# A three-block kernel's first mixer put in step order, its scan inputs ahead of q, with the shifted norms turned tile by tile and products of ones in TensorE's waits

## Chip, cores and metric

One NeuronCore of one Trainium2 chip. The metric is the device time of one execution in microseconds (us); lower is better. All data are float32, batch 1, 256 tokens, width 1024.

## The reference, cut to what matters

Nine stages run one after the other on one X of 256 x 1024: feed-forward, first mixer, feed-forward, feed-forward, second mixer, feed-forward, feed-forward, third mixer, feed-forward. The first three are normalized and then scaled and *shifted* by vectors computed from `c`; the later six have a plain norm. The change touches the three shifted norms and the first mixer.

```python
h = modulate(rms_norm(x, g_pre_mix), sh2, sc2)      # h * (1 + scale) + shift
proj = h @ w_in                                     # q 512, k 128, v 128, u 512 columns
attn = sliding_window_attention(q, k, v, sinks)     # 8 heads of 64, window 128
# state space: 32 groups of 16 channels, each a complex diagonal state of 64
bu = einsum('bsgh,gph->bsgp', u, b_bar)
states = associative_scan(a * left + right)         # over the 256 steps
y = real(einsum('bsgp,ghp->bsgh', states, c_mat)) + u * d_skip
y = gelu(y);  y = y * sigmoid(y @ w_glu + b_glu)
mixed = concat(rms_norm(attn, g_attn_out), rms_norm(y, g_ssm_out)) @ w_out
x = x + ga2 * rms_norm(mixed, g_post_mix)           # ga2: the gate of this block
```

## The kernel before, in words

**Panels.** The weights stream through a ring of six slots as panels of 128 x 1024 (`raw`). SyncE loads a panel as soon as VectorE has split the one that had its slot. ScalarE rounds it to `w_hi` (`split_hi`, line 185), VectorE takes the rest, `w_lo` (`split_lo`, line 191), and TensorE makes each product as three: hi by hi, hi by lo, lo by hi (`product3`, line 207). Activations are split alike, `h_hi` and `h_lo`. The order of the panels is fixed by hand in `stream_of_panels`, and the order in which each engine splits them, relative to its other work, is written out by hand in each stage. M1 is the mixer's first panel: 0 to 3 are u, 4 is k, 5 to 8 are q, 9 is v, 10 and 11 the GLU's weights, 12 to 19 `w_out`.

**The norm.** `add_dve` (lines 715 and 722) adds a stage's result to X; ScalarE takes squares (line 302), GpSimd the power -1/2 (lines 337, 338), VectorE writes one diagonal matrix for each half of the tokens (`diag_dve`, line 376), and `norm_turn_pe` (line 414) transposes and scales X by a matmul with the diagonal: for the first half of the tokens all eight channel tiles, then for the second half. ScalarE writes `h_hi` from PSUM with scale and shift (`norm_act_rest`, line 330), VectorE first the same in float32 into `h32` and then `h_lo` (`low_dve`, lines 394 and 396). Both wait for tiles by pairs, since two tiles share a PSUM bank. TensorE begins the first panel tile by tile as `h_lo` comes (`norm_pe`, `first_channels`, `first_up`).

**The first mixer.** TensorE (`mix1_pe`): u's first panel, projection 1, the gate of this block (`gate_pe`: ones times `acc_gate_1`, line 835, which VectorE's `gate_dve` takes up), projections 2 to 4; then four rounds of: projection 5 + b, `input_pe(b)` (line 1496, four groups of states by 64 blocks of four steps), scores of two heads (`attention_pe`, lines 1458 and 1459, banks 0 and 1); then `output_pe(0)` (lines 1506 and 1509), projection 9 (v) and its transposes (line 1538), `output_pe(1)`; then per head the transposes of the probabilities (line 1470) and the products with v (lines 1482 to 1484), with `output_pe(2)` and (3) in between. ScalarE copies each projection out (lines 1595 to 1599), gathers u by the four steps of a block into `u_steps` (`step`, line 1607, reading every fourth float), takes exponentials (line 1619), copies the turned probabilities (line 1627) and applies the Gelu (line 1633, writing every fourth float of `y32`), two groups of it ahead of `probabilities(4)`. VectorE: splits, `gate_dve`, then four times `states_dve` (lines 1742 to 1751: rotate, scan), biases and maxima of two heads (lines 1758 and 1762), a split. GpSimd turns the states back (lines 1715 to 1720), the third and fourth time only when `output_pe` has read the first and second. Then come `attention_out` (line 1788), `y_lo` (line 1813), the GLU product, Sigmoid (line 1674), the transposes of the attention, and eight `out_product`, with the sum of the gated squares (line 1568) behind the second and the row of factors (line 1440) behind the third.

Of the kernel before, what the change touches and what calls it, by code (L numbers as in the profile page):

```python
# [81 lines left out]
def build_program(nc, panels, ada, cols, rows, sinks, ssm_mats, skip, tables, pool_mats, rope, near,  # L82
                  pool_w, decay, mlp_w, feats, x_in, out, spectrum, last_stage):
    ctx = ExitStack()
    with ctx:
# [193 lines left out]
        PLAIN = 3  # L279

# [127 lines left out]

        def norm_turn_pe(pe, n):

            for m in range(MT):
                pe.wait_ge(diag_done, 2 * n + m + 1)
                for k in range(KT):
                    mm = pe.matmul(turned_out(n, k)[:, m * P:(m + 1) * P], X[:, m, k * P:(k + 1) * P],  # L414
                                   diag[:, m, :], start=True, stop=True)
                    if m == MT - 1:
                        mm.then_inc(turned, 1)

        def norm_pe(pe, n, first):
# [942 lines left out]
        u_steps = region(5120, STATE_TILES, BLOCKS)  # L1362
# [6 lines left out]
        p_turned = region(0, 2, 384)  # L1369
# [79 lines left out]
        def attention_pe(pe, i):  # L1449
# [5 lines left out]
            pe.wait_ge(m1_evac, 6 + j)  # L1455
# [57 lines left out]
        def mix1_pe(pe):  # L1513
# [23 lines left out]
            for m in range(MT):  # L1537
                tr = pe.transpose(bank[4][:, m * P:(m + 1) * P], v_t[:, m * P:(m + 1) * P], ident[:, :])
            tr.then_inc(v_turned, 1)
            output_pe(pe, 1)  # L1540
            pe.wait_ge(v_ready, 1)
            for i in range(8):
# [3 lines left out]
                if i == 3:  # L1546
                    output_pe(pe, 2)
                if i == 5:
# [13 lines left out]
            out_product(0)  # L1562
            out_product(1)
# [20 lines left out]

        def by_query(row, half, wide=2):
# [3 lines left out]
        def mix1_act(act, order):  # L1589
            def project(j):  # L1590
# [3 lines left out]
                if j < 4:  # L1594
                    ins = act.activation(u_t[:, j, :], src, ACT.Copy)
                elif 5 <= j < 9:
                    ins = act.activation(q_t[:, j - 5, :], src, ACT.Copy, scale=HD ** -0.5)
                else:
                    ins = act.activation(k_t if j == 4 else v_t, src, ACT.Copy)
                ins.then_inc(m1_evac, 1)  # L1600

            def step(b):
                if b == 0:
                    act.wait_ge(m1_evac, 4)
                    act.wait_ge(gate_sums, 4)
                for j in range(STEP):
                    act.activation(u_steps[32 * j:32 * j + 32, 4 * b:4 * b + 4, :],
                                   u_t[32 * b:32 * b + 32, :, :].rearrange("p q (t j) -> p q t j", j=STEP)[:, :, :, j],
# [40 lines left out]
            act.wait_ge(v_turned, 1)  # L1649
            act.activation(v_tok[:, :, :].rearrange("p m c -> p (m c)"), bank[4][:, 0:SEQ],  # L1650
                           ACT.Copy).then_inc(v_ready, 1)
# [1103 lines left out]
```

## Time and profile before

| | |
|---|---|
| median of 3 runs | 1647.46 us (1646.73 to 1650.32) |
| the profiled execution | 1646.31 us, its span 1644.2 us |
| mean granted TensorE clock | 0.964 of 2.4 GHz |
| TensorE matmul, weight load | 94%, 86% of the span |
| VectorE, ScalarE, GpSimd | 62%, 47%, 13% |
| chain that ended last | TensorE 83%, VectorE 8%, ScalarE 4%, issue 2%, DMA 1% |
| DMA | 293.24 MB, 178 GB/s over the span |

How to read it: the span runs from the first to the last instruction of one execution; the execution's own time is 2.1 us longer. Matmul times are pipelined and overlap (a record of 0.28 us can follow another after 0.12). One float32 matmul shows as two records. Times in a timeline are us from the span's start. The clock is the share of full speed that TensorE was granted: 1.00 is 2.4 GHz, 0.50 is 1.2 GHz.

### The profile page before, as it was taken

To read this page: it belongs to the slowest core of one execution; us is meant where nothing else is said; L and a number is where in the kernel's file an instruction comes from. 1 tells how busy PE (TensorE), PEld (TensorE's weight loads), DVE (VectorE), ACT (ScalarE), POOL (GpSimd) and SP (SyncE) were. 2 spreads that over 40 slices of the span, in tenths; PEclk is the share of its full clock that TensorE was granted. 3 is DMA by queue.
4 is the path that set the end of the run, shared out by engine and by line. 5 is a ranking of instruction groups with operands and counts; after the bars stand their busy time and mean duration, and the time that the engine had idled before them with its cause. 6 is when DMAs were issued, how large, how long until landed. Compare 5 with 4: busy or idle time off the path is not lost.

```text
span 1644.2 us, 27917 instructions
## 1 busy us (share of the span) xinstructions
PE 1539.4 (94%) x10274; PEld 1407.5 (86%) x10274; DVE 1024.8 (62%) x1379; ACT 767.7 (47%) x1211; POOL 212.9 (13%) x254
## 2 busy tenths in 40 slices
PE   3989998968899999999999999999999988999997
PEld 3989987867898888999988799999999978899996
DVE  6997776724765556655556765556655558565554
ACT  2345534654545445544454354444544456354443
POOL 1593191221101111000000000000000000000000
PEclk8999988968999999999999999999999999999999
DMA  9887863203565553855533345553655532245551
GB/s 350 303 293 273 277 254 130 81 26 128 189 199 191 205 192 118 302 188 191 191 129 105 123 158 186 190 191 131 215 191 189 177 108 102 77 167 191 190 185 47
DMA packets 80287, 293.24 MB, mean 178 GB/s; under 512 B 9035, under 2 KB 9388, under 8 KB 79644
## 3 DMA queue, kind: packets, MB, share of 16 engines
q1 hardware_dynamic: 75728, 274.97, 48.8%
q0 software_dynamic: 3712, 15.16, 2.6%
q10 hardware_dynamic: 780, 2.18, 0.5%
q8 instruction: 46, 0.75, 0.2%
q14 instruction: 21, 0.17, 0.0%
HBM read 289.13 MB, written 3.15 MB: 178 GB/s over the span
## 4 chain that ended last, share of the span: by engine, by line
PE 83%; DVE 8%; ACT 4%; issue 2%; DMA 1%; POOL 1%; SPq 0%; DVEq 0%; ACTq 0%
PE bank L207 73%; DVE w_lo L191 2%; DVE arena L774 1%; PE bank L1904 1%; PE bank L1200 1%; ACT arena L302 1%; PE bank L1917 1%; ACT w_hi L185 1%; PE bank L811 1%; PE bank L405 1%; DMA raw<-panels 1%; PE bank L1509 1%; PE bank L414 1%; DVE arena L715 1%; PE bank L1096 0%
## 5 line engine op out<-in xcount | busy, mean ns | idle before, releaser
L207 PE MATMUL bank<-h_hi,w_hi 128*128 128x256 f32 x2376 | 689.6, 290 | 17.1 <-DVE h_lo L396 5.5
L207 PE MATMUL bank<-h_lo,w_hi 128*128 128x256 f32 x2376 | 678.6, 286 | 0.0
L207 PE MATMUL bank<-h_hi,w_lo 128*128 128x256 f32 x2376 | 678.3, 285 | 0.0
L191 DVE TENSOR_TENSOR w_lo<-raw,w_hi 128x1024 fp32r<-128x1024 f32 x458 | 552.1, 1253 | 126.8 <-ACT w_hi L185 126.1
L207 PEld LDWEIGHTS bank<-h_hi,w_hi 128*128 128x128 f32 x2376 | 462.3, 195 | 35.7 <-DVE h_lo L396 7.6
L185 ACT ACTIVATE w_hi<-raw 128x1024 fp32r<-128x1024 f32 x458 | 457.4, 1049 | 65.0 <-PE bank L207 33.0
L207 PEld LDWEIGHTS bank<-h_lo,w_hi 128*128 128x128 f32 x2376 | 462.6, 195 | 6.1 <-issue 2.2
L207 PEld LDWEIGHTS bank<-h_hi,w_lo 128*128 128x128 f32 x2376 | 462.0, 194 | 0.0
L618 DVE TENSOR_TENSOR arena<-arena,bank 128x256 f32<-128x256 f32 x132 | 55.3, 419 | 249.7 <-PE bank L207 180.0
L207 PE MATMUL bank<-w_hi,f_hi 128*128 128x512 f32 x528 | 207.6, 393 | 0.2 <-DVE f_lo L623 0.2
L207 PE MATMUL bank<-w_hi,f_lo 128*128 128x512 f32 x528 | 207.0, 392 | 0.0
L207 PE MATMUL bank<-w_lo,f_hi 128*128 128x512 f32 x528 | 205.5, 389 | 0.0
L555 ACT ACTIVATE f_hi<-arena 128x256 fp32r<-128x256 f32 x132 | 55.1, 418 | 251.7 <-DVE arena L618 251.7
L337 POOL TENSOR_SCALAR stat<-stat 128x1 f32<-128x1 f32 x26 | 10.8, 417 | 1015.5 <-ACT arena L302 1014.7
L549 ACT ACTIVATE arena<-arena 128x256 f32<-128x256 f32 x88 | 36.8, 418 | 195.5 <-DVE arena L612 195.5
L207 PEld LDWEIGHTS bank<-w_lo,f_hi 128*128 128x128 f32 x528 | 99.2, 188 | 21.7
L207 PEld LDWEIGHTS bank<-w_hi,f_hi 128*128 128x128 f32 x528 | 99.6, 189 | 17.9 <-issue 0.4
L207 PEld LDWEIGHTS bank<-w_hi,f_lo 128*128 128x128 f32 x528 | 99.6, 189 | 15.7
L774 DVE SCALAR_TENSOR_TENSOR arena<-arena,stat 128x1024 f32<-128x1024 f32 x70 | 94.2, 1345 | 3.4 <-DMA arena<-ada 1.8
L623 DVE TENSOR_TENSOR f_lo<-arena,f_hi 128x256 fp32r<-128x256 f32 x132 | 59.9, 454 | 50.8 <-ACT f_hi L555 50.8
L553 ACT ACTIVATE arena<-bank 128x256 f32<-128x256 f32 x44 | 16.8, 383 | 146.3 <-PE bank L207 146.1
L207 PE MATMUL bank<-w_hi,h_hi 128*128 128x512 f32 x116 | 49.2, 424 | 7.0 <-DVE h_lo L1824 2.8
(315 smaller groups left out, 1310.0 us busy)
## 6 DMA issues: line engine op xcount, KB each, us to landing
raw<-panels SPq DMA_DIRECT2D x458, 512.0 KB, 4.7
arena<-ada SPq DMA_DIRECT2D x64, 512.0 KB, 5.2
arena<-ada POOLq DMA_DIRECT2D x8, 512.0 KB, 3.9
arena<-rows POOLq DMA_DIRECT2D x4, 512.0 KB, 4.2
spectrum<-arena POOLq DMA_DIRECT2D x2, 1024.0 KB, 7.4
arena<-spectrum POOLq DMA_DIRECT2D x1, 2048.0 KB, 19.4
X<-x_in SPq DMA_DIRECT2D x1, 1024.0 KB, 5.4
arena<-decay ACTq DMA_DIRECT2D x2, 512.0 KB, 5.7
```

The lines of the kernel that those rows point to most:

```text
L185: act.activation(w_hi[:, slot, :], raw[:, slot, :], ACT.Copy).then_inc(hi_ready, 1)
L191: dve.tensor_tensor(w_lo[:, slot, :], raw[:, slot, :], w_hi[:, slot, :].bitcast(F32), ALU.subtract).then_inc(lo_ready, 1)
L207: last = pe.matmul(out_ap, a, b, start=start and n == 0, stop=stop and n == 2)
L302: return act.activation(squares[:, q, :], source, ACT.Square, scale=D ** -0.5, accum_out=stat[:, at + q:at + q + 1])
L405: tr = pe.transpose(turned_out(n, k)[:, m * P:(m + 1) * P], X[:, m, k * P:(k + 1) * P], ident[:, :])
L414: mm = pe.matmul(turned_out(n, k)[:, m * P:(m + 1) * P], X[:, m, k * P:(k + 1) * P], diag[:, m, :], start=True, stop=True)
L549: act.activation(ffn_buf[:, f % 2, :], gate_buf[:, f % 2, :], ACT.Silu).then_inc(silu_done, 1)
L553: act.activation(ffn_buf[:, f % 2, :], gate_out(at, f), ACT.Silu).then_inc(silu_done, 1)
L555: act.activation(f_hi[:, f % 2, :], ffn_buf[:, 2 + f % 2, :], ACT.Copy).then_inc(f_hi_done, 1)
L618: dve.tensor_tensor(ffn_buf[:, 2 + f % 2, :], ffn_buf[:, f % 2, :], up_out(at, f), ALU.mult).then_inc(hidden_done, 1)
L623: dve.tensor_tensor(f_lo[:, f % 2, :], ffn_buf[:, 2 + f % 2, :], f_hi[:, f % 2, :].bitcast(F32), ALU.subtract).then_inc(f_lo_done, 1)
L774: dve.scalar_tensor_tensor(out=dst, in0=src, scalar=c, in1=dst, op0=ALU.mult, op1=ALU.add).then_inc(ada_used, 1)
```

## The change

In the shifted norms `norm_turn_pe` turns X tile by tile (both halves of the tokens of one tile, then the next), and for tiles 2, 4 and 6 ScalarE, not VectorE, writes the float32 copy `h32`. Ahead of the turns of the second and third norm TensorE multiplies 24 times ones by ones into bank 7, and in the second norm once more after each of the first seven tiles, into bank 3. In the mixer `u_t`, `y32` and what follows them stand in the order of the four steps, so that the copy out of u writes with a stride of 64 floats, and the gathering copies and the Gelus run over contiguous floats; VectorE's product `gated_y` goes back to token order, and moves from behind the first `m_lo` to ahead of it. VectorE gathers group 0, ScalarE groups 1 to 3. The q projections 5 to 8 become q, q, v, q, q (panels 5, 6, 7, 8, 9), `input_pe(0)` and (1) and `output_pe(0)` and (1) move, v's transposes go to bank 7. On ScalarE the last four probabilities stand ahead of all Gelus. The gate's two matmuls move from behind projection 1 to behind `out_product(0)`, and `gate_dve` behind the splits 16 and 17. Three of VectorE's splits move behind the second maxima.

```diff
@@ norm
+        BY_ACT = (2, 4, 6)
...
                 act.wait_ge(turned, of_channel(n, k))
+                if sh is not None and k in BY_ACT:
+                    act.activation(h32[:, k, :], turned_out(n, k), ACT.Identity, scale=sc[:, k:k + 1],
+                                   bias=sh[:, k:k + 1])
...
-                    order(dve.tensor_scalar(h32[:, k, :], ps, sc[:, k:k + 1], sh[:, k:k + 1],
-                                            ALU.mult, ALU.add))
+                    if k not in BY_ACT:
+                        order(dve.tensor_scalar(h32[:, k, :], ps, sc[:, k:k + 1], sh[:, k:k + 1],
+                                                ALU.mult, ALU.add))
...
+        def keep_busy(pe, to, times):
+            for _ in range(times):
+                pe.matmul(bank[to][:, 0:P], ones[:, :], ones[:, :], start=True, stop=True)
...
         def norm_turn_pe(pe, n):
-            for m in range(MT):
-                pe.wait_ge(diag_done, 2 * n + m + 1)
-                for k in range(KT):
+            if n:
+                keep_busy(pe, 7, 24)
+            for k in range(KT):
+                for m in range(MT):
+                    if k == 0:
+                        pe.wait_ge(diag_done, 2 * n + m + 1)
...
                 first(k)
+                if n == 1 and k < KT - 1:
+                    keep_busy(pe, 3, 1)
@@ mix1_pe
             norm_pe(pe, 1, first_channels)
-            m1_projection_pe(pe, 1)
-            gate_pe(pe, 1, acc_gate_1, (6, 7))
-            for j in range(2, 5):
+            for j in range(1, 5):
                 m1_projection_pe(pe, j)
-            for b in range(4):
-                m1_projection_pe(pe, 5 + b)
-                input_pe(pe, b)
-                attention_pe(pe, 2 * b)
-                attention_pe(pe, 2 * b + 1)
+            input_pe(pe, 0)
+            m1_projection_pe(pe, 5)
+            attention_pe(pe, 0)
+            attention_pe(pe, 1)
+            m1_projection_pe(pe, 6)
+            input_pe(pe, 1)
+            attention_pe(pe, 2)
+            attention_pe(pe, 3)
+            m1_projection_pe(pe, 7)
+            m1_projection_pe(pe, 8)
+            input_pe(pe, 2)
             output_pe(pe, 0)
+            attention_pe(pe, 4)
+            attention_pe(pe, 5)
+            pe.wait_ge(m1_evac, 8)
+            for m in range(MT):
+                tr = pe.transpose(bank[7][:, m * P:(m + 1) * P], v_t[:, m * P:(m + 1) * P], ident[:, :])
+            tr.then_inc(v_turned, 1)
             m1_projection_pe(pe, 9)
+            input_pe(pe, 3)
+            output_pe(pe, 1)
+            attention_pe(pe, 6)
+            attention_pe(pe, 7)
             pe.wait_ge(m1_evac, 10)
-            for m in range(MT):
-                tr = pe.transpose(bank[4][:, m * P:(m + 1) * P], v_t[:, m * P:(m + 1) * P], ident[:, :])
-            tr.then_inc(v_turned, 1)
-            output_pe(pe, 1)
...
-                if i == 3:
+                if i == 1:
                     output_pe(pe, 2)
-                if i == 5:
+                if i == 4:
                     output_pe(pe, 3)
...
             out_product(0)
+            pe.wait_ge(sig_done, 4)
+            gate_pe(pe, 1, acc_gate_1, (6, 7))
             out_product(1)
@@ mix1_act
-                    ins = act.activation(u_t[:, j, :], src, ACT.Copy)
+                    ins = act.activation(u_t[:, j, :].rearrange("p (j t) -> p t j", j=STEP),
+                                         src.rearrange("p (t j) -> p t j", j=STEP), ACT.Copy)
...
-                        y32[32 * b:32 * b + 32, :, :].rearrange("p q (t i) -> p q t i", i=STEP)[:, :, :, i],
+                        y32[32 * b:32 * b + 32, :, :].rearrange("p q (i t) -> p q i t", i=STEP)[:, :, i, :],
...
-            step(0)
+            act.wait_ge(u_stepped, 4)
+            step(1)
             project(4)
-            step(1)
+            step(2)
             project(5)
-            step(2)
             step(3)
-            for j in range(6, 9):
+            for j in (6, 7, 8):
                 project(j)
+            act.wait_ge(v_turned, 1)
+            act.activation(v_tok[:, :, :].rearrange("p m c -> p (m c)"), bank[7][:, 0:SEQ],
+                           ACT.Copy).then_inc(v_ready, 1)
             exps(0)
             project(9)
...
             exps(1)
-            gelu(0)
-            gelu(1)
-            probabilities(4)
-            probabilities(5)
-            gelu(2)
-            probabilities(6)
-            gelu(3)
-            probabilities(7)
+            for i in range(4, 8):
+                probabilities(i)
+            for b in range(4):
+                gelu(b)
@@ mix1_dve
-            for j in range(3):
+            for j in range(4):
                 split_lo(dve, M1 + 3 + j)
-            gate_dve(dve, 1, (6, 7), order)
-            for j in range(3, 5):
-                split_lo(dve, M1 + 3 + j)
+            dve.wait_ge(m1_evac, 4)
+            for j in range(STEP):
+                dve.tensor_copy(u_steps[32 * j:32 * j + 32, 0:4, :], of_step(0, j)).then_inc(u_stepped, 1)
+            split_lo(dve, M1 + 7)
...
-                split_lo(dve, M1 + 8 + s)
+                if s < 2:
+                    split_lo(dve, M1 + 8 + s)
             maxima(1)
-            split_lo(dve, M1 + 12)
+            for j in range(10, 13):
+                split_lo(dve, M1 + j)
...
+            for n in range(4):
+                dve.wait_ge(sig_done, n + 1)
+                dve.tensor_tensor(gated_y[:, n, :].rearrange("p (t i) -> p i t", i=STEP),
+                                  gate_in[:, n, :].rearrange("p (i t) -> p i t", i=STEP),
+                                  y32[:, n, :].rearrange("p (i t) -> p i t", i=STEP), ALU.mult).then_inc(gated, 1)
...
             dve_panels(dve, M1 + 16, 2)
+            gate_dve(dve, 1, (6, 7), order)
```

## Rows read from the trace of the kernel before

**Rows 1.** Chain of waits, 260 to 424 us: start, length, what

```profile
286.65 1.72 PE bank L835 x4
...
288.37 11.51 PE bank L207 x96
...
299.88 1.75 PE bank L1496 x16
...
369.01 8.32 PE bank L207 x48
```

**Rows 2.** Windows: us, busy of PE, PEld, DVE, ACT, POOL, clock, DMA share, GB/s

```profile
263.50:268.30 4.80, 0.00 (x0) 0.00 (x0) 4.17 (x7) 3.26 (x11) 2.25 (x5) 1.00 0.26 96
274.90:278.50 3.60, 2.48 (x12) 1.66 (x12) 3.46 (x9) 2.63 (x5) 0.00 (x0) 1.00 0.00 0
278.60:285.50 6.90, 6.90 (x28) 6.26 (x29) 4.95 (x8) 1.33 (x2) 2.10 (x2) 0.51 0.23 76
319.60:323.00 3.40, 2.77 (x21) 2.29 (x21) 3.16 (x11) 3.34 (x10) 0.00 (x0) 1.00 0.00 0
323.10:329.20 6.10, 6.10 (x28) 5.45 (x27) 5.86 (x10) 2.84 (x11) 0.00 (x0) 0.50 0.30 89
334.50:345.00 10.50, 10.25 (x92) 9.96 (x92) 1.38 (x3) 6.05 (x23) 3.91 (x4) 1.00 0.16 58
351.80:366.30 14.50, 12.20 (x54) 11.43 (x54) 0.00 (x0) 7.91 (x14) 0.00 (x0) 0.50 0.00 1
410.70:416.00 5.30, 0.00 (x0) 0.00 (x0) 4.42 (x8) 3.40 (x11) 2.65 (x6) 0.93 0.00 0
```

**Rows 3.** Timeline around the two later norms: start, length, engine, line, operation

```profile
269.68 0.29 DVE L376 TENSOR_SCALAR diag<-ident,stat 128x128 f32<-128x128 f32 x1 [0.85 <-POOL stat L338]
...
272.82 3.76 ACT L330 ACTIVATE h_hi<-bank,mods,pre_scale 128x256 fp32r<-128x256 f32 x8 [4.37 <-PE bank L414]
...
273.88 0.54 DVE L394 TENSOR_SCALAR arena<-bank,pre_scale,mods 128x256 f32<-128x256 f32 x1 [3.91 <-ACT h_hi L330]
...
281.20 1.22 DVE L191 TENSOR_TENSOR w_lo<-raw,w_hi 128x1024 fp32r<-128x1024 f32 x1
...
416.87 1.60 DVE L376 TENSOR_SCALAR diag<-ident,stat 128x128 f32<-128x128 f32 x1 [0.85 <-POOL stat L338]
...
420.75 2.39 ACT L330 ACTIVATE h_hi<-bank,mods,pre_scale 128x256 fp32r<-128x256 f32 x5 [5.11 <-PE bank L414]
...
430.29 0.39 ACT L553 ACTIVATE arena<-bank 128x256 f32<-128x256 f32 x1 [2.58 <-PE bank L207]
```

**Rows 4.** Timeline of the mixer's loop, VectorE and GpSimd

```profile
301.75 1.42 DVE L1742 TENSOR_TENSOR arena<-bank,arena 128x512 f32<-128x512 f32 x2 [2.08 <-PE bank L1496]
...
305.31 0.53 DVE L1758 SCALAR_TENSOR_TENSOR arena<-arena,bank 128x384 f32<-128x384 f32 x1
...
309.01 1.40 DVE L1742 TENSOR_TENSOR arena<-bank,arena 128x512 f32<-128x512 f32 x2
...
309.63 0.73 POOL L1720 TENSOR_TENSOR arena<-arena 128x256 f32<-128x256 f32 x1
```

**Rows 5.** Timeline of TensorE: two heads' scores; from one head's values to the next

```profile
315.41 0.50 PE L1458 MATMUL bank<-arena 64*128 64x128 f32 x4
...
316.28 0.39 PE L207 MATMUL bank<-h_hi,w_hi 128*128 128x256 f32 x1
...
339.16 0.50 PE L1470 MATMUL bank<-ident,arena 128*128 128x128 f32 x3
...
340.12 0.50 PE L1470 MATMUL bank<-ident,arena 128*128 128x128 f32 x3
```

**Rows 6.** ScalarE's groups (busy us, mean ns, idle before) and the Gelus' table load

```profile
L1633 ACT ACTIVATE arena<-bank 32x256 f32<-32x256 f32 x16 | 9.8, 612 | 6.7 <-PE bank L1509 6.4
...
L553 ACT ACTIVATE arena<-bank 128x256 f32<-128x256 f32 x44 | 16.8, 383 | 146.3 <-PE bank L207 146.1
...
344.90 1.28 ACT L1633 ACT_TABLE_LOAD   x1
```

More of the change, by code:

```diff
@@ L407, in turn_pe @@
                 tr.then_inc(turned, 1)
+        def keep_busy(pe, to, times):
+            for _ in range(times):
+                pe.matmul(bank[to][:, 0:P], ones[:, :], ones[:, :], start=True, stop=True)
         def norm_turn_pe(pe, n):
[L411 to L413 removed]
+            if n:
[4 more added lines that the diff above has]
+                        pe.wait_ge(diag_done, 2 * n + m + 1)
                     mm = pe.matmul(turned_out(n, k)[:, m * P:(m + 1) * P], X[:, m, k * P:(k + 1) * P],
                                    diag[:, m, :], start=True, stop=True)
[L416 to L417 removed]
+                mm.then_inc(turned, 1)
         def norm_pe(pe, n, first):
@@ L1361, in build_program @@
         q_t = region(1024, 4, SEQ)
-        u_steps = region(5120, STATE_TILES, BLOCKS)
+        u_steps = region(0, STATE_TILES, BLOCKS)
         y32 = region(4096, 4, SEQ)
@@ L1368, in build_program @@
         turned_states = (region(8704, 2, SEQ), region(9216, 2, SEQ))
-        p_turned = region(0, 2, 384)
+        p_turned = region(10752, 2, 384)
+        gated_y = region(11264, 4, SEQ)
         attn = region(3072, 2, 512)
@@ L1454, in attention_pe @@
             b = bank[i % 2]
-            pe.wait_ge(m1_evac, 6 + j)
+            pe.wait_ge(m1_evac, (6, 7, 9, 10)[j])
             if i >= 2:
@@ L1583, in turn_attention_pe, with of_step @@
                     tr.then_inc(attn_turned, 1)
+        def of_step(b, j):
+            return u_t[32 * b:32 * b + 32, :, :].rearrange("p q (j t) -> p q j t", j=STEP)[:, :, j, :]
         def by_query(row, half, wide=2):
@@ L1594, in project @@
                 if j < 4:
-                    ins = act.activation(u_t[:, j, :], src, ACT.Copy)
-                elif 5 <= j < 9:
-                    ins = act.activation(q_t[:, j - 5, :], src, ACT.Copy, scale=HD ** -0.5)
+                    ins = act.activation(u_t[:, j, :].rearrange("p (j t) -> p t j", j=STEP),
+                                         src.rearrange("p (t j) -> p t j", j=STEP), ACT.Copy)
+                elif j in (4, 7):
+                    ins = act.activation(k_t if j == 4 else v_t, src, ACT.Copy)
                 else:
-                    ins = act.activation(k_t if j == 4 else v_t, src, ACT.Copy)
+                    ins = act.activation(q_t[:, (5, 6, 8, 9).index(j), :], src, ACT.Copy, scale=HD ** -0.5)
                 ins.then_inc(m1_evac, 1)
             def step(b):
-                if b == 0:
-                    act.wait_ge(m1_evac, 4)
-                    act.wait_ge(gate_sums, 4)
                 for j in range(STEP):
-                    act.activation(u_steps[32 * j:32 * j + 32, 4 * b:4 * b + 4, :],
-                                   u_t[32 * b:32 * b + 32, :, :].rearrange("p q (t j) -> p q t j", j=STEP)[:, :, :, j],
+                    act.activation(u_steps[32 * j:32 * j + 32, 4 * b:4 * b + 4, :], of_step(b, j),
                                    ACT.Copy).then_inc(u_stepped, 1)
@@ L1686, in mix1_act @@
                 act.wait_ge(gated, n + 1)
-                act.activation(y_squares[:, n, :], gate_in[:, n, :], ACT.Square).then_inc(gsq_done, 1)
+                act.activation(y_squares[:, n, :], gated_y[:, n, :], ACT.Square).then_inc(gsq_done, 1)
             act_panels(act, M1 + 18, 2)
@@ L1825, in mix1_dve @@
                                   ALU.subtract).then_inc(m_lo, 1)
-            for n in range(4):
-                dve.wait_ge(sig_done, n + 1)
-                dve.tensor_tensor(gate_in[:, n, :], gate_in[:, n, :], y32[:, n, :],
-                                  ALU.mult).then_inc(gated, 1)
             dve_panels(dve, M1 + 16, 2)
+            gate_dve(dve, 1, (6, 7), order)
             dve.wait_ge(gsum_done, 1)
@@ L1836, in mix1_dve @@
             for n in range(4):
-                dve.scalar_tensor_tensor(out=h32[:, 4 + n, :], in0=gate_in[:, n, :],
+                dve.scalar_tensor_tensor(out=h32[:, 4 + n, :], in0=gated_y[:, n, :],
                                          scalar=col("g_ssm", n), in1=bank[4][:, 0:SEQ], op0=ALU.mult,
@@ L2610, in mix1 @@
         q = w[:, :512].reshape(D, 2, 4, HD).transpose(0, 2, 1, 3).reshape(D, 512)
-        return [columns(w[:, 768:]), columns(w[:, 512:640]), columns(q), columns(w[:, 640:768]),
+        return [columns(w[:, 768:]), columns(w[:, 512:640]), columns(q[:, 0:256]), columns(w[:, 640:768]),
+                columns(q[:, 256:]),
                 together(columns(a["ssm_w_glu"][0]), 2), a["w_out"][0].reshape(8, P, D)]
```

3 lines of the change are left out of this document (removed).

## The prediction

> **What bounds the kernel now.** I read the page's share of busy time first (TensorE 94%), then the chain of waits, the windows, and the timeline of each engine from 262 to 431 us, the part that the diff touches. Past it TensorE multiplies almost without a break, so what is gained before passes to the end one for one. In the chain [rows 1] the reader is to see four projections in 11.51 us, 2.88 each, then `input_pe(0)`, 16 records in 1.75, and the GLU product only at 369.01: 67 us lie between. In the windows [rows 2] the granted clock is 0.50, the 1.2 GHz level, in 278.6 to 285.5, 323.1 to 329.2 and 351.8 to 366.3, each time after a stretch in which TensorE had gaps. The norm [rows 3] is paced by VectorE: eight tiles from 273.88 to 281.20, 0.915 each. The mixer's loop is VectorE's too [rows 4]: 301.75 to 309.01, 7.26 a step, of which the states take 3.56, two heads 2.3, a split 1.4. Last, two groups of Gelus stand on ScalarE ahead of probabilities that TensorE waits for.
>
> **The norm ahead of the mixer.** The turn went token half by token half, so ScalarE began at 272.82, with tiles 0 and 1 whole. Now these need six records after the second diagonal, ready at 269.68 + 0.29 [rows 3]. A float32 matmul is two records, and the gate's two took 1.72 as four records of 512 columns [rows 1], 0.107 per 128 columns. 270.0 + 0.64 + 0.15 to drain: ScalarE starts at 270.8. It needs 3.76 for eight tiles, about 0.45 each; with three copies more it ends at 275.9. VectorE starts 1.05 after it, as now, and loses three instructions of 0.57 (273.88 to the next in the pair): 271.9 + 7.3 - 1.7 = 277.5 for the last `h_lo`, and ScalarE is never later than it wants. TensorE ends projection 0 at 278.0.
>
> The 24 products of ones are 48 records, 5.1 us at the full clock. They fill an idle time (263.5 to 268.3: no TensorE [rows 2]); at the half clock they would take 10.2 and end 4.9 late. The single product in each later wait costs 0.21 and stands in waits of 0.3 to 0.5; where ScalarE made the copy the tile comes after 0.35 and it may delay 0.2, which the next tile gives back. I take it that all this holds the clock: the fall at 278.5 came after 3.6 us in which TensorE was busy for 2.48. Without the half clock, and without the gate's 1.72, projections 1 to 4 run from 278.0 to 289.5 and `input_pe(0)` to 291.3, where it ended at 301.6: 10.3 gained. The group 0 copies of u, now VectorE's, are ready at about 288.5 (projection 3 ends at 286.65, ScalarE's copy out takes 0.4 to 0.65, VectorE's four 0.2 to 0.4 each); projection 4 hides them with 1 us in hand, and beyond that they would cost one for one. ScalarE's copy of u now writes with a stride, between 0.38 and 0.61 each [rows 6]; it stands beside projections of 2.88 and costs nothing.
>
> **The loop.** ScalarE waits for VectorE's copies (288.5); behind that wait stand its step 1 and split 7, so VectorE's split 7 ends at 292.2 and the first states begin there, 9.5 earlier. From here the two engines alternate. TensorE: projection 5 to 294.2, two heads after the copy of q, 0.87 (315.41 to 316.28 [rows 5]), projection 6, `input_pe(1)`: 300.3. VectorE: step 0 to 299.5, step 1 from 300.3, heads done 306.2, split 307.6. TensorE: heads, projections 7 and 8, `input_pe(2)`: 300.3 + 0.9 + 5.76 + 1.75 = 308.7; `output_pe(0)` (24 records of 0.11) 2.6, heads 0.9, v 0.4, projection 9, `input_pe(3)`: 317.3. VectorE: states(3) to 320.9, two heads to 323.3. GpSimd turns a group of states 4.9 after its scan (305.4 to 310.36 [rows 4]); it waits for `output_pe(0)` before group 2, and that now ends at 311.3, ahead of states(2): no `output_pe` waits. SyncE refills a slot when VectorE has split it: splits 10 to 12 move behind the maxima, to 327 to 330, and their loads are for panels used after 360. ScalarE's wait for v holds up the Exps to 314.4; they end at 318.2, q's last copy at 319.7, and TensorE comes for it at 320.0.
>
> **The values.** TensorE has two heads to turn, and then nothing until the eighth head leaves the score banks at 323.3. What follows are `output_pe(2)` and (3), 2.6 each, and eight heads of values at 0.96 (339.16 to 340.12 [rows 5]): 12.9, with waits the last product at 336.7. At 1.2 GHz the same is 5.2, 5.2 and eight times 1.92, less 0.7 done before the gap, with waits of 1: the last product at about 347.5. Nearest rows [rows 2]: 319.6 to 323.0, busy 2.77 of 3.4 with narrow products, and 0.50 straight after; 351.8 to 366.3, busy 12.2 of 14.5, stayed at 0.50. Against them 334.5 to 345.0 held 1.00, but without gaps (10.25 of 10.5). With a gap of near 2 us I take the half clock. The Trainium skill (TensorE: Matmul & The Clock Gate, section Why this matters for your kernels) asks only that TensorE have no long idle gap between bursts; by that rule the clock stays full here, the last product is at 336.7 and the total 1622. The window at 319.6 speaks against it: no long gap stood there and the clock fell.
>
> **The Gelus.** They come last: a table load 1.28, then 16 at 612 ns as now, or 383 as a ScalarE function of 256 contiguous elements out of PSUM [rows 6]; the diff makes their writes contiguous, so I take the nearer row, 383, back to back 0.33: 5.3 in all. Bounds: 4.8 and 10.2 (0.64 each, today's spacing). With `y_hi`, two of 512 columns at 0.6 (between once and twice 383), and two `y_lo` of 0.35 behind it: 345.5 + 1.3 + 5.3 + 1.2 + 0.8 = 354.1 for the GLU, against 369.01. **Gain 14.9.** It contains the 10.3 of the front.
>
> **The tail.** The gate's 1.72 now stands behind `out_product(0)`, on TensorE's way to the sum of squares, the row and the last products: **cost 1.7**, nothing hides it. Its wait for the Sigmoids is over by then. VectorE's gating moves ahead of `m_lo`; it needs 0.5 after the last Sigmoid (bounds 0.42 and 0.65 for its strided write), and `m_hi` comes over 1 us later.
>
> **The second norm.** Here the second diagonal took 1.60 [rows 3], beside GpSimd's load and memset, so 418.5. ScalarE can start at 419.25, against 420.75. Then TensorE's 48 products (5.8) are slower than VectorE's tiles: first Silu at 427.6 against 430.29, gain 2.7 at the full clock. But here TensorE goes idle at 410.7 (410.7 to 416.0: nothing [rows 2]), the ones end 5.1 later, and nearly 3 us with little to do follow; a fall there costs 2.4 of the 2.7. I take **1.5**. The first norm gains nothing: its six products a tile last longer at the half clock (1.28) than VectorE's 0.915.
>
> **Sum.** -14.9 + 1.7 - 1.5 = -14.7. The profiled execution took 1646.31: 1631.6. The median is 1.15 higher, so **1632.5 us**.
>
> **Rivals.** *Full clock in the values*: GLU at 344.5, 24.5 earlier; +1.7, -2.7: -25.5, 1622. The window 334.5 to 345.0 is for it. So is the rule of the Trainium skill named above. Chance 0.20. *The Gelus stay at 0.64*, because of their 32 partitions or the function: +4.9, 1637. The trace has no contiguous one. 0.13. *An earlier fall*, between 307 and 321: a projection, an input and an output at half, 2.9 + 1.75 + 2.6, less waits: +5, 1637.5. 0.15. *Slower than before*: the half clock comes with `input_pe(0)` at 289.5 and stays to the GLU. Five projections cost 14.4 more, four inputs 7.0, two outputs 5.2, four pairs of heads 3.5; less 3 of waits, 27: -14.7 + 27, 1660. It turns the sign once more than 15 of these 27 are paid. Against it: four projections in a row ran at the full 2.88 after just such a half stretch [rows 1]. 0.04. *Nothing comes of it*: GpSimd or the Exps take VectorE's place, within 3 us. 0.02.
>
> **Numbers.** My own case has 0.46 and spans 1628 to 1636. For 8 in 10 the range goes to the full clock on one side, and on the other to where a dear Gelu or an early fall comes with a late wait or two: 1621 to 1641. A measurement of this kernel tells 0.2%, 3.3 us, from no change. Faster 0.94, within 0.02, slower 0.04.
>
> **What would show it.** Right: clock 1.00 from the mixer's first product to about 320 and 0.50 from 323 to the GLU; the first `h_hi` 2 us earlier; `input_pe(0)` over by 291.5; the Gelus at 0.38; GLU at 354; a step of 1.7 behind `out_product(0)`. Wrong: a wait for VectorE or ScalarE ahead of a projection between 292 and 317, products of ones at 0.21 a record, or values at 0.11 per narrow record.

## The result, and the profile after

The changed kernel takes **1636.33 us** in the median of four runs (1634.08 to 1638.84); the kernel before, run beside it, 1647.86 (1646.73 to 1650.32). The ratio is 0.9929 (95% interval 0.9916 to 0.9942): 11.5 us faster. Two executions of this case, one of `no_ones` (3020.16 us) and one of the kernel before (2171.43), fell in a much slower state and are left out everywhere. The forecast was 1632.5 in a range of 1621 to 1641; the prediction's own case spans 1628 to 1636, and the median lies 0.3 above it. The execution shown below took 1634.08 (span 1632.3), 12.2 less than the one shown of before.

The page of the changed kernel: its busy time by engine, and the granted clock in 40 slices.

```profile
PE 1542.5 (94%) x10384; PEld 1415.1 (87%) x10384; DVE 1024.4 (63%) x1374; ACT 762.8 (47%) x1216; POOL 211.4 (13%) x254
...
PEclk7999989959999999999999999999999988999999
```

The shares tell nothing: TensorE was and is 94% busy. The clock row does: the ninth slice (327 to 367 us) is at 5, and two slices of the last mixer (1306 to 1388) are at 8.

The chain of waits of the changed kernel, from the first mixer's norm to the second norm (start us, us, what), the lines that answer to [rows 1, 3]:

```profile
270.22 0.30 DVE diag L380
...
270.57 3.62 PE bank L427 x30
...
278.48 9.10 PE bank L207 x75
...
287.61 0.65 ACT arena L1626
...
299.78 1.73 PE bank L1511 x16
...
314.02 1.17 DVE arena L1797
...
315.21 1.30 DVE arena L1799 x2
316.53 0.72 DVE arena L1801
...
322.08 0.27 ACT arena L1631
...
325.23 0.41 PE bank L1497 x2
...
345.99 1.28 ACT L1661
...
355.81 8.55 PE bank L207 x48
...
372.58 1.72 PE bank L849 x4
...
386.67 9.19 PE bank L207 x39
...
404.09 1.61 DVE diag L380
...
405.75 5.24 PE bank L427 x30
```

The reader is to see the GLU product at 355.81 instead of 369.01 [rows 1], the gate's 1.72 at 372.58 in the tail, and VectorE's operations of four and eight elements of `maxima(0)` (L1797 to L1801), 1.3 us a pair where the same pair of L1799 takes 0.23 in `maxima(1)`, in the chain to the last copy of q (L1631), for which TensorE waited.

The windows of the changed kernel (columns as in [rows 2]):

```profile
318.00:322.40 4.40, 3.24 (x31) 3.11 (x29) 4.16 (x8) 4.34 (x17) 0.00 (x0) 1.00 0.00 0
322.40:327.30 4.90, 3.88 (x33) 3.33 (x33) 4.45 (x9) 0.87 (x2) 3.91 (x4) 1.00 0.00 0
327.30:348.00 20.70, 20.08 (x98) 19.70 (x96) 4.23 (x8) 8.51 (x26) 0.00 (x0) 0.50 0.22 77
348.00:355.80 7.80, 0.00 (x0) 0.00 (x0) 2.72 (x7) 7.43 (x19) 0.00 (x0) 0.50 0.00 1
355.80:361.50 5.70, 5.69 (x26) 5.69 (x27) 4.25 (x5) 4.53 (x8) 2.50 (x4) 0.50 0.50 172
...
405.90:409.30 3.40, 3.40 (x17) 3.40 (x18) 0.93 (x3) 1.33 (x3) 1.07 (x2) 0.51 0.65 213
```

From the norm to 327.3 the clock is 1.00; from there through all the values, the wait for the Gelus and most of the GLU it is 0.50, the 1.2 GHz level.

Kernels whose code ahead of this part is the same start it up to 6.4 us apart in their profiles (`norm_only` at 259.67, `early_q` at 266.07), since the part ahead of it varies. So I compare stages by their length, each the difference of two times of the timeline: first square of the feedforward's result (A), last `h_lo` of the mixer's norm (B), end of `input_pe(0)` (C), second product of the first head's values, in `attention_out_pe(0)` (D; the first product starts 0.24 us earlier in the changed kernel), last value product (E), GLU product (F), first square behind the mixer (G), first Silu (H). The kernels of the section on experiments stand in the same table, one profiled execution each.

| kernel | A-B | B-C | C-D | D-E | E-F | F-G | G-H | A-H |
|---|---|---|---|---|---|---|---|---|
| before | 19.84 | 20.32 | 37.11 | 27.50 | 2.79 | 39.66 | 21.62 | 168.84 |
| changed | 16.24 | 13.92 | 33.30 | 22.43 | 7.91 | 40.07 | 20.90 | 154.77 |
| norm_only | 16.27 | 18.51 | 35.49 | 27.51 | 2.80 | 39.72 | 20.89 | 161.19 |
| mixer_only | 20.58 | 13.93 | 33.96 | 13.82 | 8.92 | 39.29 | 21.62 | 152.12 |
| no_ones | 17.87 | 13.93 | 34.23 | 24.25 | 7.93 | 40.81 | 21.54 | 160.56 |
| fill_wait | 16.26 | 13.91 | 33.30 | 17.99 | 7.94 | 37.44 | 20.89 | 147.73 |
| gate_front | 16.26 | 15.64 | 33.29 | 13.83 | 8.90 | 37.47 | 21.18 | 146.57 |
| gate_front_no_ones | 17.88 | 15.63 | 33.29 | 22.74 | 7.92 | 39.63 | 20.88 | 157.97 |
| ones_front | 16.24 | 15.71 | 34.23 | 24.25 | 7.91 | 39.28 | 19.27 | 156.89 |
| gelu_stride | 16.26 | 13.93 | 33.30 | 22.71 | 11.71 | 39.62 | 20.73 | 158.26 |
| early_q | 16.25 | 13.93 | 31.26 | 18.11 | 7.91 | 39.49 | 20.76 | 147.71 |
| early_fill | 16.25 | 13.93 | 31.63 | 17.45 | 8.44 | 35.93 | 20.85 | 144.48 |
| best | 16.24 | 15.64 | 31.64 | 13.42 | 6.95 | 35.78 | 20.89 | 140.56 |
| best_no_fill | 16.26 | 15.64 | 31.25 | 13.42 | 6.39 | 40.07 | 20.89 | 143.92 |

Between A and H the change is worth 14.1 us. The profile shown started A 0.56 later than that of before, so 13.5 were left at the first Silu (416.78 against 430.29), and 11.9 of the span at the end. The rest was given back far behind the change. Windows of the changed kernel and then of the kernel before, where the last mixer runs at the half clock:

```profile
1334.50:1344.60 10.10, 6.77 (x30) 6.48 (x31) 6.79 (x11) 4.63 (x5) 0.00 (x0) 0.50 0.15 54
1361.70:1371.90 10.20, 9.29 (x27) 7.21 (x27) 6.66 (x13) 5.35 (x15) 0.00 (x0) 0.50 0.01 2
```

```profile
1350.50:1357.30 6.80, 3.75 (x18) 3.46 (x17) 5.16 (x9) 4.63 (x5) 0.00 (x0) 0.50 0.12 25
1418.70:1422.10 3.40, 3.30 (x13) 3.00 (x13) 2.69 (x5) 1.90 (x4) 0.00 (x0) 0.50 0.00 0
```

The code there is the same; 20 us at the half clock stand against 10. By the chain the changed kernel was 14.85 ahead at the first products of that mixer (1324.75 against 1339.60) and 11.87 at its last norm (1430.72 against 1442.59). All fourteen traces of this case hold this unchanged code. From the row of factors ahead of those products to the turn of that norm, its length goes with its time at the half clock: 103.6 us in the kernel before (10.2 us at 0.50), 104.0 to 104.8 in four others (13.7 or 17.1 us), 106.5 to 106.9 in the nine with 20.5 us, the changed kernel among them.

### The profile page after: what moved, and what is told of

Its sections match the earlier page's. It is cut to its first block, busy times and chain, and to the rows that moved or that the text cites. A ratio compares the mean times of both kernels' runs of the same rounds, so it can differ in the third digit from the quotient of the medians.

```text
span 1632.3 us, 28136 instructions
## 1 busy us (share of the span) xinstructions
PE 1542.5 (94%) x10384; PEld 1415.1 (87%) x10384; DVE 1024.4 (63%) x1374; ACT 762.8 (47%) x1216; POOL 211.4 (13%) x254
## 4 chain that ended last, share of the span: by engine, by line
PE 83%; DVE 7%; ACT 4%; issue 2%; DMA 1%; POOL 1%; SPq 0%; DVEq 0%; ACTq 0%
PE bank L207 73%; DVE w_lo L191 2%; DVE arena L788 1%; PE bank L1933 1%; PE bank L1214 1%; DMA arena<-ada 1%; ACT arena L303 1%; ACT w_hi L185 1%; PE bank L2262 1%; PE bank L1946 1%; POOL stat L342 1%; PE bank L410 1%; PE bank L427 1%; PE bank L2284 1%; PE bank L825 1%
```

## The experiments

Twelve kernels ran, those of one group on one chip with the kernel before between them (its medians there: 1646.32 to 1648.86), so that kernels of two groups compare better by their ratios and stages than by their medians. All compute the whole reference; a product of ones is one whose result nobody reads. The ratios are as recorded; where times fall in two groups, they can differ from the quotient of the medians (0.9915 for `no_ones`).

| kernel | median us (runs) | ratio to before, 95% interval |
|---|---|---|
| changed | 1636.33 (4) | 0.9929, 0.9916 to 0.9942 |
| no_ones | 1633.55 (6) | 0.9900, 0.9885 to 0.9914 |
| norm_only | 1638.09 (5) | 0.9942, 0.9930 to 0.9955 |
| mixer_only | 1634.62 (6) | 0.9925, 0.9908 to 0.9943 |
| fill_wait | 1631.83 (5) | 0.9906, 0.9892 to 0.9920 |
| gate_front | 1626.78 (4) | 0.9878, 0.9861 to 0.9896 |
| gelu_stride | 1641.18 (1) | one run, no interval |
| early_q | 1630.02 (4) | 0.9895, 0.9878 to 0.9913 |
| early_fill | 1625.60 (4) | 0.9879, 0.9861 to 0.9897 |
| ones_front | 1634.28 (6) | 0.9914, 0.9892 to 0.9936 |
| gate_front_no_ones | 1640.17 (6) | 0.9950, 0.9934 to 0.9965 |
| best | 1620.72 (5) | 0.9835, 0.9819 to 0.9851 |
| best_no_fill | 1623.33 (5) | 0.9850, 0.9836 to 0.9863 |

**The change in two halves.** `norm_only` is the kernel before with the norm's part of the diff (`BY_ACT`, `keep_busy`, `norm_turn_pe`, `norm_pe`) and nothing else; `mixer_only` the changed kernel without that part.

> The kernel before with the norm part of the change alone (turn tile by tile, ScalarE's copies for tiles 2, 4, 6, products of ones). Theory A (front first): the last h_lo near 277.5, the clock held at 1.00 through the first projections, some 7 us gained before input_pe(0) that old loop passes on, and 1 to 2 at the norm behind the mixer: 1639 to 1641. Theory B (the old order of the mixer, paced by VectorE's gate and splits, eats it): 2 to 4 us gained, 1644 to 1646, and the mixer part holds the rest.

> The changed kernel with the norms as they were before (token half by token half, no copies by ScalarE, no products of ones). Theory A: the clock falls near 268 and 278 as before, the front loses about 7 us against the changed kernel, the second norm 1.5 to 2.5: 1643 to 1645. Theory B (the step order carries the gain): 1638 to 1641.

Measured: 9.4 us gained by the norm alone and 12.9 by the mixer alone, while both together gave 11.5. They do not add. The table shows why. The norm's part is worth 3.6 us in A-B on the kernel before and 4.3 on `mixer_only`; the mixer's part 6.4 in B-C on the kernel before, 1.7 of it the gate. But `mixer_only`, which has the half clock at its norm, runs its values in 13.82 and the changed kernel in 22.43. Windows of `mixer_only`:

```profile
270.50:277.00 6.50, 6.05 (x28) 6.05 (x29) 0.89 (x3) 1.39 (x5) 2.70 (x6) 0.50 0.35 114
277.30:328.20 50.90, 47.01 (x382) 43.92 (x381) 39.59 (x67) 26.61 (x56) 15.71 (x14) 1.00 0.23 73
328.40:331.50 3.10, 3.03 (x14) 1.98 (x14) 2.16 (x4) 0.52 (x2) 2.40 (x2) 0.50 0.00 0
331.80:345.80 14.00, 12.91 (x114) 12.53 (x114) 5.63 (x12) 7.63 (x25) 1.29 (x2) 1.00 0.34 114
```

The clock falls at the wait for the last copy of q (328.2), a little ahead of where it fell in the changed kernel, but it is back after 3.1 us, where the changed kernel stays down for 34. Of `mixer_only` theory A's fall at the norm came, and with it 4.3 us in A-B, yet the time of 1634.62 lies below even theory B's 1638 to 1641: neither had the values at the full clock. Of `norm_only` theory A held in kind, with 5.4 us gained by the end of `input_pe(0)` where it said some 7, and 1638.09 just under its 1639 to 1641.

**The products of ones.**

```
-            if n:
-                keep_busy(pe, 7, 24)
...
-                if n == 1 and k < KT - 1:
-                    keep_busy(pe, 3, 1)
```

> The changed kernel without any product of ones (neither the 24 ahead of a turn nor the single ones in the waits); all outputs stay as they are. Theory A (the ones hold the clock): the granted clock falls to 0.50 near 268 and again near 278, stays there for about 7 us of the first projections, and 3.4 us are lost there; at the norm ahead of the dense layer 0 to 2 more. 3 to 6 us slower than the changed kernel, 1639 to 1642. Theory B (the turn tile by tile and the lack of the gate are enough to keep the clock): no fall between 262 and 320, within 1 us of the changed kernel.

Measured: the half clock came, 272.3 to 278.8, and A-B grew by 1.6; so far theory A. But the kernel was not slower; by the recorded ratios it was even faster (0.9900 against 0.9929). Its six times were 1629.80, 1630.93, 1632.47, 1634.62, 1642.17 and 1643.70, on both sides of the changed kernel's; the profiled one, of 1643.70, has the values at 0.50 too:

```profile
272.30:278.80 6.50, 5.78 (x25) 5.49 (x26) 2.50 (x7) 2.50 (x5) 2.64 (x6) 0.50 0.39 114
279.00:326.70 47.70, 45.99 (x386) 44.08 (x385) 36.17 (x60) 26.77 (x56) 15.70 (x14) 1.00 0.25 78
327.00:355.00 28.00, 26.84 (x127) 25.63 (x127) 8.44 (x17) 9.10 (x28) 3.91 (x4) 0.50 0.16 57
```

The low times have no trace, but every execution has its mean granted clock on record: 0.963 to 0.967 for the four below 1635, 0.956 and 0.957 for the two above 1642. By that the low ones spent some 28 us less at the half clock (0.0085 x 2 x 1635, an estimate). That these 28 us lie in and behind the values is likely (with the same mixer D-E is 13.82 in `mixer_only` and 24.25 here) and not shown.

**The two waits ahead of the values.** In the changed kernel TensorE waited 1.16 us for the last copy of q and 1.02 for the eighth head's bias, and at 327.3 the clock fell.

```
             output_pe(pe, 1)
+            pe.wait_ge(bu_read, 3)
+            keep_busy(pe, 2, 5)
             attention_pe(pe, 6)
...
                 attention_values_pe(pe, i)
+                if i == 1:
+                    keep_busy(pe, 2, 5)
```

> The changed kernel with ten more products of ones on TensorE, whose result nobody reads: five ahead of attention_pe(6), where it waited 1.16 us for the last copy of q, five ahead of attention_out_pe(0), where it waited 1.02 us for the eighth head's bias. Theory A (the two gaps bring the half clock): the clock stays 1.00 past 327, the last value product comes 7 to 10 us before 348, and the time is 1626 to 1630. Theory B (the narrow products of 64 columns bring it whatever the gaps): the clock falls within 2 us of 327 as now, and the time is within 1 us of the changed kernel's 1636.

Measured: 4.5 us under the changed kernel in the medians, 3.8 by the ratios, whose intervals just touch. It is as theory A has it at half the size: with the start 1.8 later the fall came at 336.2, and only the end of the values is at 0.50:

```profile
322.70:327.30 4.60, 4.60 (x40) 4.02 (x40) 4.17 (x9) 2.35 (x6) 2.20 (x2) 1.00 0.00 0
327.30:335.90 8.60, 7.52 (x69) 7.38 (x69) 5.52 (x10) 4.44 (x18) 1.72 (x3) 1.00 0.43 149
336.20:345.30 9.10, 9.09 (x45) 8.90 (x44) 0.41 (x2) 3.67 (x7) 0.00 (x0) 0.50 0.05 21
```

D-E is 17.99 instead of 22.43, 4.4 us shorter, and F-G another 2.6. With narrow products from 327.3 to 335.9 the clock stayed at 1.00 here; theory B, a fall near 327 whatever the gaps, falls.

**The gate's place.**

```
+            m1_projection_pe(pe, 1)
+            gate_pe(pe, 1, acc_gate_1, (6, 7))
-            for j in range(1, 5):
+            for j in range(2, 5):
...
-            pe.wait_ge(sig_done, 4)
-            gate_pe(pe, 1, acc_gate_1, (6, 7))
```

(and `gate_dve` back behind VectorE's third split)

> The changed kernel with the gate's two products and VectorE's part of it back behind the second projection, where they were before. Theory A (in the tail nothing hides the gate, in the front nothing hides it either): GLU product to first Silu 1.7 us shorter than in the changed kernel (60.97), last h_lo to input_pe(0) 1.7 longer (12.03), and the time within 1 us of 1636. Theory B (VectorE's gate of 1.3 us delays the splits and the scan inputs): the front loses 3 us or more, the time is 1638 or more.

Measured: 1626.78, 9.5 us faster than the changed kernel in the medians and 8.4 by the ratios, where theory A expected nothing and theory B a loss. B-C is 1.72 longer, as expected. A-H is 8.2 shorter all the same: F-G by 2.60 (1.72 of it the gate's own, the rest a shorter half stretch in the GLU), and D-E by 8.60, 13.83 against 22.43, the values at the full clock; E-F is 0.99 longer, G-H 0.28. And the waits ahead of them were there as before. Windows of `gate_front`:

```profile
325.00:329.30 4.30, 2.12 (x18) 1.46 (x17) 3.91 (x8) 2.09 (x5) 2.16 (x2) 1.00 0.00 0
329.30:343.20 13.90, 12.79 (x114) 12.42 (x113) 5.97 (x12) 7.48 (x24) 1.75 (x3) 1.00 0.33 115
343.20:352.00 8.80, 0.00 (x0) 0.00 (x0) 2.69 (x6) 8.39 (x21) 0.00 (x0) 0.67 0.00 1
352.00:356.20 4.20, 4.12 (x19) 4.12 (x20) 3.52 (x4) 4.18 (x8) 1.40 (x2) 0.50 0.36 116
```

TensorE is busy for 2.12 of 4.30 us, C-D is the same 33.3, and the clock stays at 1.00 until the long wait for the Gelus. So the same gaps in the same order can be followed by either clock. What differs in the program is what ran some 40 us earlier; besides, each execution meets this part at another time. I tested whether it is the gate or the time that TensorE is busy with it:

```
             m1_projection_pe(pe, 1)
+            keep_busy(pe, 3, 8)
```

> The changed kernel with eight products of ones (1.71 us), whose result nobody reads, behind the second projection, where the gate's two products (1.72 us) stood before; the gate itself stays in the tail. Theory A (where TensorE's 1.7 us stand in time shifts the fall of the clock; the gate's own place matters little): the fall near 327 comes past 340, the values run at 1.00, and the time is 1627 to 1631. Theory B (the gate in the tail, or VectorE's part of it, cost the 9 us between the changed kernel and gate_front): the clock falls near 329 as in the changed kernel, and the time is 1636 to 1639.

Measured: neither. Six times in two groups, 1630.34, 1630.80, 1631.83 and 1636.73, 1638.90, 1640.29: three near theory A's times, three near B's. The profiled one (1638.90) is of the upper group, and its clock fell ahead of the last copy of q:

```profile
318.00:325.20 7.20, 6.66 (x59) 6.53 (x58) 6.89 (x12) 5.57 (x19) 3.25 (x4) 1.00 0.00 0
325.50:354.00 28.50, 27.30 (x128) 25.98 (x128) 8.47 (x17) 9.58 (x29) 3.90 (x4) 0.50 0.15 56
```

So the same program can come out either way. The lower three have no trace; their mean granted clock is 0.970 or 0.971, that of the upper three 0.962 to 0.965, some 23 us less at the half clock (an estimate as above). The last test of this group takes the norms' ones out of `gate_front`:

> gate_front without any product of ones in the norms. Theory A (the norm's ones are worth the half stretch at the front): the clock is 0.50 from about 272 to 279, the last h_lo 1 us later, and the time 2 to 4 us above gate_front's 1626.8. Theory B (the later falls decide, and they move with the earlier ones): a time that differs by up to 8 us in either direction, or two groups of times, with a first fall near 272 in the profile all the same.

Measured: 1640.17, all six within 1636.95 to 1641.13: 13.4 us slower than `gate_front` (11.9 by the ratios), more than theory A's 2 to 4, and one group instead of theory B's two. By the stages: 1.62 in A-B, which is the half stretch at the norm, 8.91 in D-E and 2.16 in F-G. The norm and the values:

```profile
270.50:277.20 6.70, 5.96 (x26) 5.67 (x27) 2.69 (x7) 2.56 (x6) 2.65 (x6) 0.50 0.39 111
332.00:353.00 21.00, 20.48 (x98) 20.11 (x97) 4.31 (x9) 8.39 (x26) 0.06 (x1) 0.50 0.22 76
```

The same products of ones that gained nothing in the median where the gate is late are worth 12 us where it is early. What they buy is mostly not the 7 us of clock beside them but the next fall, 60 us on.

**The Gelus' stride.**

```
-  y32[32 * b:32 * b + 32, :, :].rearrange("p q (i t) -> p q i t", i=STEP)[:, :, i, :]
+  y32[32 * b:32 * b + 32, :, :].rearrange("p q (t i) -> p q t i", i=STEP)[:, :, :, i]
```

> The changed kernel with the Gelus writing y32 with the stride of 4 elements of before (and the gating without its rearrangement). Theory A (the contiguous write is what made a Gelu 0.37 instead of 0.61): 16 Gelus take 10.2 us instead of 6.35, and the GLU product comes 3.9 later. Theory B (they are faster for another reason, such as standing back to back): 6.4 us as now.

Measured: theory A. The line's durations (min/median/max ns), first of the changed kernel, then of `gelu_stride`:

```profile
L1661 ACT ACTIVATE arena<-bank x16: 371/374/378, 347.3 to 353.3; 32x256 f32<-32x256 f32 x16
```

```profile
L1661 ACT ACTIVATE arena<-bank x16: 606/610/618, 351.4 to 360.9; 32x256 f32<-32x256 f32 x16
```

16 times 0.236 is 3.8, and E-F grew by 3.8 (7.91 to 11.71).

**A better order.** `early_q` moves ScalarE's last copy of q ahead of the Exps and TensorE's heads 6 and 7 ahead of `output_pe(1)`, takes the first half of the second Exps earlier, puts VectorE's `maxima(0)` ahead of states(2) and the last biases and `maxima(1)` ahead of states(3), and `output_pe(3)` one head later:

```
-            output_pe(pe, 1)
             attention_pe(pe, 6)
             attention_pe(pe, 7)
+            output_pe(pe, 1)
...
-            exps(0)
+            exp_sink(0)
             project(9)
+            exps(0, range(4))
...
-                if s == 2:
-                    maxima(0)
...
+                if s == 1:
+                    maxima(0)
             maxima(1)
+            states_dve(dve, order, 3)
```

`early_fill` adds 4 products of ones ahead of `attention_out_pe(0)` and 32 behind the last value product. `best` is `early_fill` with the gate in front, `output_pe(3)` moved to the eighth head, and VectorE's splits 11 and 12 behind states(3) and the sums of the Exps; `best_no_fill` is `best` without those 36.

> The changed kernel with the end of the mixer's loop in another order: ScalarE copies the last q ahead of the Exps and takes the second half's Exps earlier, TensorE turns heads 6 and 7 ahead of output_pe(1), VectorE takes maxima(0) ahead of states(2) and the last two biases and maxima(1) ahead of states(3); output_pe(3) one head later. Theory A (the wait for the eighth head's bias, and the half clock behind it, set the GLU's start): attention_out_pe(0) near 322.5 instead of 325.2, no fall near 327, the last value product near 336, GLU product near 345: 1625 to 1629. Theory B (ScalarE's Exps, copies and Gelus are the bound anyway, or the clock falls as before): GLU not earlier than 352, 1632 to 1637.

> The kernel early_q with 36 more products of ones, whose result nobody reads: 4 ahead of attention_out_pe(0), 32 (6.8 us at the full clock) behind the last value product, where TensorE waits some 8 us for the Gelus. Theory A (a wait of 8 us brings the half clock for the GLU): the clock stays 1.00 through the GLU product, which takes 6 instead of 8.5 us, and the time is 2 to 4 us below early_q. Theory B: within 1 us of early_q.

> gate_front and early_fill together, with output_pe(3) behind the last head's transposes and VectorE's splits 11 and 12 behind states(3), beside nothing of GpSimd. Theory A (clock held to the GLU, ScalarE's Gelus the bound): attention_out_pe(0) near 325, last value product 8 us behind it, last h_lo to GLU product 66 to 68 us against 71.5 in early_fill and 71.7 in gate_front, 1619 to 1623. Theory B (the clock falls in the values anyway): 70 us or more, 1624 to 1628.

> The kernel best without its 36 products of ones in the values and behind the last of them (those of the norms stay). Theory A (a wait of 6 to 7 us behind the last value product brings the half clock for the GLU): last h_lo to last value product as in best (60.7), the clock 0.50 from within the wait or shortly behind it, GLU product to first Silu 2 to 4 us longer: 1623 to 1625. Theory B (the order alone holds the clock): within 1 us of best's 1620.7. Theory C (already the 0.5 to 1 us wait ahead of attention_out_pe(0) brings the fall): values at 0.50, 1628 or more.

Measured: `early_q` 1630.02. C-D was 2.0 shorter, but the fall came at 337.8 in the values and the GLU was at 353.5, with the start of this part 4.1 later than in the changed kernel: theory A's first half only. `early_fill` 1625.60, 4.4 less: the fall came at 333.1 in the values, the clock was back at 343.3 in the products of ones, and with the GLU at 1.00 F-G was 3.6 shorter. The price is a little above theory A's 2 to 4; that the clock would stay up is not what happened. `best` 1620.72, the fastest of all, and the steadiest, 1620.05 to 1622.31: B to F is 67.6 us (15.64 + 31.64 + 13.42 + 6.95), as theory A had it. Windows of `best`:

```profile
320.00:326.00 6.00, 6.00 (x56) 5.60 (x55) 4.50 (x13) 4.11 (x18) 1.25 (x2) 1.00 0.27 87
326.00:339.00 13.00, 12.21 (x112) 11.97 (x111) 4.88 (x9) 9.01 (x27) 3.91 (x4) 1.00 0.24 83
339.00:345.80 6.80, 6.80 (x63) 6.80 (x63) 3.16 (x7) 6.53 (x15) 0.00 (x0) 1.00 0.01 4
345.80:352.00 6.20, 6.20 (x54) 6.20 (x54) 4.75 (x7) 4.83 (x10) 2.50 (x4) 1.00 0.65 225
```

There is no half clock from 250 to 371 us. `best_no_fill` took 1623.33, 2.6 more (2.5 by the ratios): the values as in `best` (13.42), then the fall in the wait (343.3), and F-G 4.3 longer, less 0.6 in E-F: theory A. In that profile of `best` the ones behind the last value product ended 0.6 us after the last `y_lo` (345.29; the GLU product at 345.88) and so cost that much of E-F; they gave back over four.

## Why the prediction was right, and where not

The direction and the range held, 11.5 us gained where 14.7 to 15 were forecast, and the norm and the projections went as its mechanism says. That the values ran at the half clock, on which the number rests, was in part luck, as told below.

**The norm**: A-B fell by 3.60, from 19.84 to 16.24; the prediction had 3.8. ScalarE's first tile came at 271.54, 270.98 less the later start, for 270.8. Right. That ScalarE's copies carry a share of it was not tried by itself.

**Projections and first input**: B-C 13.92, against 291.3 - 277.5 = 13.8. Right, and the clock held through it as said.

**The loop**: two terms were missing. `maxima(0)` has no time of its own in my working; it took 3.6 us (313.64 to 317.24) beside GpSimd's turn of the states. And ScalarE loads a table behind the copy of v, 1.28 us from 314.40, so that the Exps could not have started before 315.7 in any case. They started at 317.3 for 314.4, the last copy of q ended at 322.35 for 319.7, and TensorE waited for it. From C to the first product of the values it took 33.1 us where my times give 32.1 (291.3 to 323.4): cost 1.0.

**The values**: the half clock came as predicted, and from the first value product to the last it took 22.7 us for my 24.1. The step behind it is where the reasoning failed: "With a gap of near 2 us I take the half clock." `fill_wait`, with the gaps filled, kept the full clock some 7 us longer (to 336.2, less the start 1.8 later), which speaks for their part in it; `gate_front` shows that the same gaps can pass at 1.00. The argument could not tell the two outcomes apart, so that the half clock came was in part luck, and the rival at the full clock was not as far off as 0.20 says: it is what `gate_front` runs. The Trainium skill (TensorE: Matmul & The Clock Gate, section Why this matters for your kernels) asks that no long idle gap stand between bursts. Of the changed kernel the trace disagrees (waits of 1.16 and 1.02 us, and 34 us at 0.50); of `gate_front` and `best` it agrees.

**The Gelus**: 6.35 for 5.3. A duration of 0.374 was nearly my row's 0.383, but they follow each other at 0.397, not 0.33. Mis-sized by 1.05; the stride as the reason is shown.

**The tail**: "cost 1.7, nothing hides it" is the row at 372.58, 1.72. Right as a price, and in front it costs the same (B-C 15.64 in `gate_front` against 13.92). F-G grew by 0.41 only, since the kernel before had a half stretch in its last products (10.75 us for 9.19 now). What I missed is that the place of these 1.7 us in time moved the clock's fall, which is worth five times their price.

**The second norm**: G-H fell by 0.72 for a predicted 1.5, inside the bounds 0.3 and 2.7. The products of ones did not hold the clock: it fell at 405.9 in the turn.

**Passing to the end**: "what is gained before passes to the end one for one" held within 1.4 us up to 1324 and failed in the last mixer, where 3 us were lost to longer stretches of the half clock in unchanged code.

**Sum**: 14.9 - 1.7 + 1.5 was predicted, 12.2 came in the profiled execution. The GLU was 13.2 earlier, 1.7 short of the forecast: 0.56 the later start, 0.3 up to C, 1.0 in the loop, 1.3 the Gelus and what stands behind them, less 1.4 in the values. The second norm was 0.8 short, F-G 1.3 better than the gate's price, and 1.6 went behind the first Silu: 14.7 - 1.7 - 0.8 + 1.3 - 1.6 = 11.9 of the span.

**What stays open**: why the clock falls at 327 in one execution and not in the other. The stages ahead of it are equally long in the changed kernel and `gate_front` (C-D 33.30 and 33.29), and `ones_front` comes out both ways. Whether a state carried from earlier falls decides it, as `gate_front_no_ones` suggests, was not isolated. The Trainium skill (TensorE: Matmul & The Clock Gate, section What's actually happening) says that the chip's watch over TensorE runs freely, not from the kernel's start, so that how many of one kernel's matmuls run at the half clock varies between runs. The two groups of times and mean clocks of `ones_front` and `no_ones` agree with that; no run here isolates it. Nor was it tried to start this part earlier or later with the same program.

## What to carry to other kernels

A stage of small products with waits between them can take 22.4 us instead of 13.8, and whether it does can hang on an edit 40 to 60 us earlier; so judge an edit near such a stage by the granted clock of every stage of the new trace, and by several executions, not by its own price. Filling TensorE's waits with products that nobody reads paid 2.6 us where it covered the whole wait between the values and the GLU (`best` against `best_no_fill`); ahead of the norm it was worth nothing or 12 us, depending on where the gate stood. `best`, with the gate in front, the better order and these products together, is 15.6 us under the changed kernel and within 2.3 us from run to run. Write strided outputs contiguous and let later, longer instructions reorder them: that alone was 3.8 us here.

## What was unexpected of the hardware

- The same waits on TensorE (busy 2.12 of 4.30 us) at 1.00 in `gate_front`, and ones like them (7.12 of 9.30 us, 318.0 to 327.3) with 34 us at 0.50 behind them in the changed kernel.
- How long it stayed down after a fall ahead of or in the first values: 3.1 us in `mixer_only` (328.4 to 331.5), 34 in the changed kernel, through 20 us with TensorE busy for 20.08 of 20.70.
- A ScalarE function on 32 partitions of 256 elements takes 374 ns with a contiguous output and 610 with a stride of 4 elements.
- VectorE operations of 4 or 8 elements a partition take 0.14 to 0.17 us alone. Of the six of `maxima(0)` three took 1.16, 1.22 and 0.71 us beside GpSimd's operations of 512 and 256 elements, and each of the three ended within 0.03 us of the end of one of these: 3.6 us for the six (313.64 to 317.24), against 1.0 for the six of `maxima(1)` in `early_fill` (320.86 to 321.89), where GpSimd was idle.
